# The first stage of a two-block network kernel: the condition's row from identity and columns, x loaded first, table products among the tiles, gate items between splits

## The reference, cut to what matters

```python
def modulation(c, w, b):
    return jnp.split(jax.nn.silu(c) @ w + b, 3, axis=-1)

def sandwich(x, mod, g_pre, g_post, fn):
    shift, scale, gate = mod
    h = rms_norm(x, g_pre) * (1.0 + scale[:, None]) + shift[:, None]
    return x + gate[:, None] * rms_norm(fn(h), g_post)

def mixer(h, j=j):                       # layer 0
    u, qr, fr, vr, gr = jnp.split(h @ hyb_w_in[j], split_at, axis=-1)
    y = jnp.concatenate([pool_mixer(u, pool_w[j], pool_scale[j]),
                         hgrn2_mixer(qr, fr, vr, gr, lower_bounds[j], hgrn_out_norm[j])], axis=-1)
    return y @ hyb_w_out[j]
```

## Time and profile before

| | us |
|---|---|
| median of 3 runs | 1265.91 |
| lowest, highest | 1264.04, 1266.17 |
| the profiled execution | 1265.72 |
| its span in the profile | 1263.9 |

### The profile page before, as it was taken

The page is one execution under the profiler, slowest core; times in us unless marked ns, Lnnn a source line. Parts: engine busy times, 40 slices in busy tenths (PEclk is TensorE's granted clock), DMA queues, the critical chain, the costliest instruction groups (busy, mean ns, idle before and its releaser), DMA issues.

```text
span 1263.9 us, 20420 instructions
## 1 busy us (share of the span) xinstructions
PE 1232.8 (98%) x7846; PEld 1115.0 (88%) x7846; DVE 922.9 (73%) x1198; ACT 719.5 (57%) x1068; POOL 63.0 (5%) x116
## 2 busy tenths in 40 slices
PE   7899999999999999999999999999999999999999
PEld 4788899999999778999989989888888888888888
DVE  6989888886897558666676695576666777666665
ACT  4576744444744557444466764655555667655554
POOL 1111011110121000000001000000000000000000
PEclk8999999999999999999999999999999999999999
DMA  8987789995699625565546544456665552365650
GB/s 323 394 319 258 278 308 332 329 325 200 235 389 392 206 44 167 200 201 201 202 161 228 168 147 154 127 192 205 204 205 204 176 174 95 121 217 204 199 166 34
DMA packets 145903, 274.39 MB, mean 217 GB/s; under 512 B 5463, under 2 KB 86383, under 8 KB 145704
## 3 DMA queue, kind: packets, MB, share of 16 engines
q1 hardware_dynamic: 130380, 220.43, 50.7%
q0 software_dynamic: 14256, 50.94, 11.2%
q10 hardware_dynamic: 1196, 2.04, 0.4%
HBM read 272.30 MB, written 1.10 MB: 216 GB/s over the span
## 4 chain that ended last, share of the span: by engine, by line
PE 85%; DVE 8%; ACT 3%; issue 2%; DMA 2%; ACTq 0%; SPq 0%; DVEq 0%
PE ps L2285 83%; DVE wlo L1340 2%; DMA raw<-in_ada_t 1%; ACT whi L576 1%; DVE raw L1368 1%; PE ps L2719 1%; DMA ada_ring<-in_ada_w 1%; DVE ada_ring L1368 1%; DVE acc_a L1361 0%; DMA vtab<-in_vtab 0%; PE ps L2449 0%; PE ps L2466 0%; DVE x L1452 0%; DVE h L1443 0%; DVE rs L2005 0%
## 5 line engine op out<-in xcount | busy, mean ns | idle before, releaser
L1340 DVE TENSOR_TENSOR wlo<-raw,whi 128x1024 fp32r<-128x1024 f32 x400 | 486.6, 1223 | 237.4 <-ACT whi L576 236.7
L576 ACT CAST whi<-raw 128x1024 fp32r<-128x1024 f32 x400 | 416.5, 1048 | 392.4 <-PE ps L2285 387.9
L2285 PE MATMUL ps<-hboth,whi 128*128 128x256 f32 (+1 forms) x2720 | 605.9, 311 | 1.1 <-DVE hboth L1569 0.5
L2285 PE MATMUL ps<-hboth,wlo 128*128 128x256 f32 x1792 | 491.9, 274 | 0.4 <-DVE wlo L1340 0.2
L2285 PEld LDWEIGHTS ps<-hboth,whi 128*128 128x128 f32 x2720 | 448.7, 191 | 30.3 <-issue 5.7
L2285 PEld LDWEIGHTS ps<-hboth,wlo 128*128 128x128 f32 x1792 | 344.3, 192 | 2.6 <-ACT whi L576 0.5
L2285 PE MATMUL ps<-whi,hboth 128*128 128x512 f32 (+1 forms) x512 | 158.4, 379 | 14.8 <-DVE hboth L1394 9.9
L2285 PE MATMUL ps<-whi,hidhi 128*128 128x512 f32 x434 | 164.5, 379 | 0.0
L2285 PE MATMUL ps<-wlo,hidhi 128*128 128x512 f32 x434 | 164.1, 378 | 0.0
L2285 PE MATMUL ps<-whi,hidlo 128*128 128x512 f32 x434 | 164.1, 378 | 0.0
L2285 PEld LDWEIGHTS ps<-whi,hboth 128*128 128x128 f32 x512 | 96.3, 191 | 31.2 <-issue 17.6
(11 more groups left out here) (266 smaller groups left out, 1108.8 us busy)
## 6 DMA issues: line engine op xcount, KB each, us to landing
raw<-in_ffn_w_in SPq DMA_DIRECT2D x44, 1024.0 KB, 5.2
raw<-in_w_mlp_up SPq DMA_DIRECT2D x32, 1024.0 KB, 5.3
raw<-in_w_mlp_down SPq DMA_DIRECT2D x32, 1024.0 KB, 4.9
ada_ring<-in_ada_t POOLq DMA_DIRECT2D x48, 512.0 KB, 6.2
raw<-in_ffn_w_out SPq DMA_DIRECT2D x22, 1024.0 KB, 4.9
raw<-in_att_w_qkv SPq DMA_DIRECT2D x18, 1024.0 KB, 8.9
raw<-in_w_in_even SPq DMA_DIRECT2D x18, 1024.0 KB, 4.9
ada_ring<-in_ada_w POOLq DMA_DIRECT2D x32, 512.0 KB, 6.5
```

The lines of the kernel that those rows point to most:

```text
L576: A.copy(whi[:, H % 4, :], raw[:, slot(n), h * HALF:(h + 1) * HALF]).then_inc(s["hi_ready"], 1)
L1340: V.tensor_tensor(wlo[:, H % 4, :], raw[:, slot(n), h * HALF:(h + 1) * HALF], whi[:, H % 4, :].bitcast(F32), ALU.subtract).then_inc(s["lo_ ...
L2285: return pe.matmul(out, lhsT, rhs, start=first, stop=last, skip_group_check=True)
```

## The change

The computation stays as it is; its order and some of its places change.

- SP loads x first. `voh` follows behind the second chunk's modulation weights.
- The identity's arrival is counted with the columns' (`cols_in`), and the silu waits for both. VectorE builds `spread` directly behind that silu, before the small steps on the columns, and no longer waits for `voh` and `vtab`.
- TensorE makes the two products of the row first. VectorE copies the row in two halves, each when its product is done. The warming products (`warm_ones`, line 2552 of before in the same function) become 12, 5, 3 and 3 instead of 12 and 6.
- ScalarE squares x in two instructions of 1024 columns, one for each half of the rows, and takes the root at once (`rsqrt`), without `mean_x` on VectorE.
- The table products stand behind tile 3 (two) and tile 5 (two). ScalarE copies them out, in chunk 5 and after chunk 6's activations, and writes them to memory there.
- `band` and `pool_w` are loaded behind split 7 instead of split 3, `masks` behind the first evacuation. Space in the on-chip memory is laid out so that these loads do not overlap the tables.
- POOL starts its gate loads when all eight modulation loads are used, not seven.
- On VectorE each split from 10 to 15 follows one gate item. On ScalarE splits 12 to 15 stand between the steps that prepare the recurrence.

```diff
-ROW_STEP = 4
+ROW_STEP = 1
...
-            sp.dma_start(voh[:, :], t["voh"]).then_inc(s["const_in"], 16)
             sp.dma_start(x[:, :, :], t["x"][0].rearrange("(t p) n -> p t n", p=P)).then_inc(s["x_in"], 16)
...
+                if at == 2:
+                    sp.dma_start(voh[:, :], t["voh"]).then_inc(s["const_in"], 16)
...
-            pool.wait_ge(s["ada_used"], ADA_FIRST - 1)
+            pool.wait_ge(s["ada_used"], ADA_FIRST)
...
-            act.dma_start(ident[:, :], t["ident"]).then_inc(s["const_in"], 16)
+            act.dma_start(ident[:, :], t["ident"]).then_inc(s["cols_in"], 16)
             act.dma_start(vtab[:, :], t["vtab"]).then_inc(s["const_in"], 16)
-            act.wait_ge(s["cols_in"], 16)
+            act.wait_ge(s["cols_in"], 32)
...
-            norms(0)
+            act.wait_ge(s["x_in"], 16)
+            for tt in range(2):
+                r = small[:, 5, 3 + tt:4 + tt]
+                A.activation(xn1[:, tt, :], x[:, tt, :], ACT.Square, accum_out=stat[:, 4 + tt:5 + tt]) \
+                    .then_inc(s["ssq_x"], 2)
+                act.wait_ge(s["ssq_x"], 2 * tt + 2)
+                rsqrt(r, stat[:, 4 + tt:5 + tt], 1.0 / D, s["act_step"], tt + 1, s["root_x"])
...
+            def table_row(g):
+
+                act.wait_ge(s["vec_dil"], 3 + g)
+                A.activation(vrow[:, g * VLEN_DIL:(g + 1) * VLEN_DIL], ps[0:8, 4 + g % 2, 0:VLEN_DIL], ACT.Copy,
+                             scale=1.0 / DIL_SCALE).then_inc(s["vec_dil_c"], 1)
...
-                if k == 3:
-                    act.wait_ge(s["vec_out"], 32)
+                if k == 5:
+                    table_row(0)
+                    table_row(1)
+                if k == 7:
                     act.dma_start(bandqk[:, :], t["band"]).then_inc(s["band_in"], 16)
                     act.dma_start(poolw[:, :, :], t["pool_w"][0].rearrange("g c d -> c g d")).then_inc(s["band_in"], 16)
-                    act.dma_start(masks[:, :, :], t["masks"]).then_inc(s["band_in"], 16)
...
-            dve.wait_ge(s["const_in"], 48)
-            spread = h321[:, :, :].rearrange("p a b -> p (a b)").rearrange("p (k n) -> p k n", k=KD)
-            link(V.tensor_tensor(spread, bcast(ident[:, :], KD), sc[:, :].unsqueeze(2).to_broadcast([P, KD, P]),
-                                 ALU.mult))
...
+            for nh in range(2):
+                dve.wait_ge(s["vec_dil"], nh + 1)
+                ins = V.tensor_copy(scrow[:, nh * 512:(nh + 1) * 512], ps[:, 6 + nh, :])
...
-            gate_items(0, acc_a, range(4))
-            split(10)
-            split(11)
-            gate_items(0, acc_a, range(4, 8))
-            for q in range(4):
-                split(2 * (FIRST["hyb_in"] + 4) + 4 + q)
-                if q == 1:
-                    col_items(1, range(2))
+            for k in range(6):
+                gate_items(0, acc_a, (k,))
+                split(10 + k)
+            gate_items(0, acc_a, (6, 7))
+            col_items(1, range(2))
...
+                if k == 3:
+                    pe.wait_ge(s["const_in"], 32)
+                    for g in range(2):
+                        mm(ps[0:8, 4 + g, 0:VLEN_DIL], vtab[:, 8 * g:8 * g + 8],
+                           voh[:, g * VLEN_DIL:(g + 1) * VLEN_DIL]).then_inc(s["vec_dil"], 1)
...
-            pe.wait_ge(s["band_in"], 48)
+            pe.wait_ge(s["band_in"], 32)
```

More of the change, by code:

```diff
@@ L131, in program @@
                 h321 = sb(r, "h321", [P, 2, 512])
+                sb(r, "past_poolw", [P, 26 * 256])
                 vtab = sb(r, "vtab", [33, 24 + 8])
@@ L840, in _ @@
                              scale=scol[:, 0, k:k + 1]).then_inc(s["hhi_ready"], 1)
+                if k == 6:
+                    table_row(2)
+                    act.wait_ge(s["vec_dil"], 3 + DG)
+                    A.copy(vrow[:, 3 * VLEN_DIL:], ps[0:8, 5, :]).then_inc(s["vec_dil_c"], 1)
+                    act.wait_ge(s["vec_dil_c"], 4)
+                    act.dma_start(t["vec_dil"].rearrange("g h n -> h g n"),
+                                  vrow[:, 0:3 * VLEN_DIL].rearrange("h (g n) -> h g n", g=3)).then_inc(s["vec_out"], 16)
+                    act.dma_start(t["vec_swa"], vrow[:, 3 * VLEN_DIL:]).then_inc(s["vec_out"], 16)
             act.wait_ge(s["lb_step"], 1)
@@ new lines, in _ @@
+            split(8)
+            split(9)
+            evac(0, KD, "A", HYB[0][2], f1, tok1)
+            act.dma_start(masks[:, :, :], t["masks"]).then_inc(s["cols_in"], 16)
+            evac(1, KD, "B", HYB[1][2], f1, tok1)
+            split(10)
+            split(11)
+            act.wait_ge(s["vec_out"], 32)
+            act.wait_ge(s["proj_free"], 2)
+            A.activation(sq1[:, :, :].rearrange("p a b -> p (a b)"), fl[:, 1024:2048], ACT.Sigmoid,
+                         scale=-1.0).then_inc(s["sig_ready"], 1)
@@ new lines, in _ @@
+            split(12)
+            act.wait_ge(s["sig_ready"], 1)
+            A.activation(fl[:, 1024:2048], fl[:, 1024:2048], ACT.Sigmoid).then_inc(s["sig_ready"], 1)
+            tables(SILU)
+            split(13)
+            act.wait_ge(s["pool_d"], 1)
+            A.copy(pooled[:, :, :].rearrange("p a b -> p (a b)"), flat(6)).then_inc(s["pool_dc"], 1)
+            act.wait_ge(s["lb_done"], 1)
+            act.wait_ge(s["sig_ready"], 2)
+            for h in range(HL):
+                a = h * S
+                A.activation(bandqk[:, 1024 + a:1024 + a + S], sq1[:, h, :], ACT.Copy, scale=small[:, 4, 4 + h:5 + h])
+                ins = A.activation(fl[:, 1024 + a:1024 + a + S], fl[:, 1024 + a:1024 + a + S], ACT.Identity,
+                                   bias=small[:, 4, h:h + 1], scale=small[:, 4, 4 + h:5 + h])
@@ L874, in _ @@
+            ins.then_inc(s["hg_prep"], 1)
+            split(14)
+            evac(2, 2 * FIRST["hyb_in"] + 12, HYB[2][0], HYB[2][2], f1, tok1)
             act.wait_ge(s["proj_free"], 3)
             A.activation(fl[:, 0:1024], fl[:, 0:1024], ACT.Silu).then_inc(s["sig_ready"], 1)
+            split(15)
             act.wait_ge(s["pool_y"], 1)
@@ L2551, in warm_ones @@
                 for _ in range(n):
-                    mm(ps[:, 4, 0:P], ones[:, :], ones[:, :])
+                    mm(ps[:, 0, 0:P], ones[:, :], ones[:, :])
             def first_tile(k):
@@ L2570, in _ @@
             warm_ones(12)
-            pe.wait_ge(s["const_in"], 48)
-            for g in range(DG):
-                mm(ps[0:8, g, 0:VLEN_DIL], vtab[:, 8 * g:8 * g + 8], voh[:, g * VLEN_DIL:(g + 1) * VLEN_DIL]) \
-                    .then_inc(s["vec_dil"], 1)
-            mm(ps[0:8, 3, :], vtab[:, 24:32], voh[:, 3 * VLEN_DIL:]).then_inc(s["vec_dil"], 1)
             pe.wait_ge(s["dve_step"], ROW_STEP)
@@ L2578, in _ @@
             for nh in range(2):
-                m = mm(ps[:, 6 + nh, :], ones[:, :], spread[:, nh * 512:(nh + 1) * 512])
-            m.then_inc(s["vec_dil"], 1)
-            warm_ones(6)
+                mm(ps[:, 6 + nh, :], ones[:, :], spread[:, nh * 512:(nh + 1) * 512]).then_inc(s["vec_dil"], 1)
+            warm_ones(5)
             pe.wait_ge(s["xn_ready"], 1)
@@ L2588, in _ @@
                     .then_inc(s["turned"], 1)
-            pe.wait_ge(s["vec_dil_c"], 4)
+            warm_ones(3)
             for k in range(KD):
                 first_tile(k)
+                if k == 3:
[3 more added lines that the diff above has]
+                           voh[:, g * VLEN_DIL:(g + 1) * VLEN_DIL]).then_inc(s["vec_dil"], 1)
+                elif k == 5:
+                    pe.wait_ge(s["vec_dil_c"], 2)
+                    mm(ps[0:8, 4, 0:VLEN_DIL], vtab[:, 16:24], voh[:, 2 * VLEN_DIL:3 * VLEN_DIL]) \
+                        .then_inc(s["vec_dil"], 1)
+                    mm(ps[0:8, 5, :], vtab[:, 24:32], voh[:, 3 * VLEN_DIL:]).then_inc(s["vec_dil"], 1)
+            pe.wait_ge(s["vec_dil_c"], 4)
             for h in range(2):
```

62 lines of the change are left out of this document (13 added, 49 removed).

## The result

The changed kernel takes 1267.38 us in the median (1266.78 to 1268.77, 10 runs), the kernel before 1264.11 beside it (1263.23 to 1268.16, 10 runs). The ratio is 1.0021, with a 95% interval of 1.0014 to 1.0029: slower by about 2.7 us. Forecast was 1261.0. The profiled execution of after took 1267.37 us, with a span of 1265.6 (before: 1265.72 and 1263.9).

A forecast was written before the change was run, and what follows sets the result against it. Up to the first level it took the chain as bound by the `vtab` load and TensorE, then VectorE, then transfers. Profiled 1265.7 less 4.8 gained there is 1260.9; with the median 0.2 above, forecast 1261.0, range 1258.0 to 1263.7.

The forecast's parts named there:

- the routes: Chunks' end to first level: VectorE's work to 72.1, ScalarE's to 74.5 to 76, transfers' to 78.4; latest counts, 77.8 taken.
- the sizes between 1.98 and 3.78: Row's two products on TensorE before the first chunk: 3.64 us at half clock, 1.8 at whole; 3.6 taken.

The follow-up runs named there:

- e1_band_early: The changed kernel with the loads of `band` and `pool_w` back at split 3 instead of 7; 1266.47 us, ratio 1.0014 to the kernel before.
- e3: The changed kernel with the identity loaded by SP ahead of x, not by ScalarE behind the columns; 1263.79 us, ratio 0.9994 to the kernel before.
- e7: The changed kernel with the identity loaded by SP ahead of x and splits 10 to 15 in their old places; 1262.17 us, ratio 0.9974.
- e8: e7 with `band` and `pool_w` loaded at split 3 instead of 7; 1263.09 us, ratio 0.9985 to the kernel before.
- e11: e7 with POOL's gate loads started when seven modulation loads are used, not eight; 1264.82 us, ratio 0.9999 to the kernel before.
- e14: e7 with `band` and `pool_w` loaded at split 5 instead of 7; 1262.52 us, ratio 0.9985 to the kernel before.
- e10: The changed kernel with 22 warming products instead of 12 at the start; 1265.98 us, ratio 1.0008 to the kernel before.
- e6: The changed kernel with `voh` loaded first again and x second; 1265.18 us, ratio 0.9998 to the kernel before.
- e9: The changed kernel with `voh` loaded first again, x second, and splits 10 to 15 in their old places; 1262.73 us, ratio 0.9987.
- e4: The changed kernel with `EARLY` 4 instead of 3, so SP may issue each projection load one load earlier; 1267.37 us, ratio 1.0026.
- e2: The changed kernel with splits 10 to 15 back in their old places on VectorE and 12 to 15 on ScalarE; 1265.36 us, ratio 1.0005.
- e13: The changed kernel with only VectorE's splits 10 to 15 back in their old places; 1265.12 us, ratio 1.0001 to the kernel before.
- e12: The changed kernel with only ScalarE's splits 12 to 15 back in their old place; 1268.36 us, ratio 1.0026 to the kernel before.

## What to carry to other kernels

When a small transfer becomes the head of the critical path, look at what every queue issues within the microsecond around it: large loads moved half a microsecond ahead cost it 1.8 to 3.4 us here, and loading it ahead of everything on their queue was the cure. An in-order engine on which independent work is shuffled item by item waits at each item for the latest of all sources; put the work whose input may be late behind what is ready, and sum the routes with their meetings, not apart. When an early gain meets a stretch in which the DMA engines are full, moving one load forward takes from another. Before calling the transfers the bound, look whether they are full right ahead of the point that is late.

## What the runs showed of the hardware

The row's two products (four instructions) show how TensorE's clock answered to its idle time ahead of them. In after and in e1_band_early (stretches of a microsecond, columns as above) the granted clock falls like this:

```profile
9.00:10.00 1.00, 0.34 (x1) 0.33 (x2) 0.93 (x4) 0.99 (x2) 0.00 (x0) 0.94 1.05 389
10.00:11.00 1.00, 1.00 (x2) 0.34 (x1) 0.41 (x3) 0.97 (x3) 0.00 (x0) 0.50 1.07 393
```

```profile
9.00:10.00 1.00, 0.58 (x2) 0.34 (x3) 0.90 (x5) 0.99 (x2) 0.00 (x0) 1.00 1.06 389
10.00:11.00 1.00, 1.00 (x3) 0.49 (x2) 0.54 (x3) 0.94 (x4) 0.00 (x0) 0.67 1.10 406
11.00:12.00 1.00, 1.00 (x2) 0.34 (x1) 0.36 (x1) 1.00 (x3) 0.00 (x0) 0.50 1.02 401
```

0.50 is 1.2 of 2.4 GHz. The products took 1.88 to 1.93 us without a gap ahead of them (e3, e7, e8, e11, e14), 1.98 after 0.57, 0.67 and 1.75 us of idleness (e10, e6, e9), 2.60 after 2.45 (e4), 2.91 after 2.77 (e1), 3.39 after 3.34 (e2), 3.61 after 3.04 (after), and 3.78 after 3.78 and 3.85 (e13, e12). In the kernel before, the clock was at 0.50 by 8 to 10 us behind 1.14 us of idleness, when TensorE had the table's products; so the idle time alone doesn't tell it, and what else counts stays open. I hadn't expected the sizes between 1.98 and 3.78. The stretches show where they come from: in e1 the products begin at 9.42 at the full clock, which falls while they run, with TensorE busy again; in e13, with 3.78 us of idleness, it is down to 0.55 at 8 to 9 us, before they begin. The longer the engine had stood still ahead of them, the more of them ran at half (if not in strict order), and a fall seen in a stretch can so belong to idleness before it. And the 64 KB of the identity landed by 3.1 us as the first load on SP's queue, at 4.7 and 6.3 on ScalarE's with `voh` ahead of x (e6, e9, the same order of loads), and at 7.6 to 8.1 with x first.
